# A two-block transformer kernel: joined products in a recurrence, and a reordered tail

## The reference

```python
# mixer: a matrix-memory attention group and a delta-rule recurrence, forward and backward (2 directions z)
q, k = silu(mq), silu(mk) * D_HM ** -0.5          # after a convolution
out_m = sigmoid(mo) * headnorm(mlstm(q, k, v, gates))
def step(state, inp):                              # the recurrence, per head, 512 positions
    removed = einsum('zhvk,zhk->zhv', state, kh_t)
    state = state * w_t - removed[..., None] * (kh_t * a_t) + v_t[..., None] * k_t
    return state, einsum('zhvk,zhk->zhv', state, r_t)
x = layernorm(ALPHA * x + g1 * (mixed @ w_out)) * gain + bias
h = modulate(x)                                    # another layer norm
# experts: 4 groups of 8; the best group, in it the best two experts of each token
w = softmax(two best) * p_group
# tokens sorted by expert, padded to blocks of places, each block with one expert's weights
y = (silu(xb @ gate[e]) * (xb @ up[e])) @ down[e] * w
x = layernorm(ALPHA * x + g2 * sum(y)) * gain + bias
```

## Time and profile before

| what | before |
|---|---|
| median of 3 runs | 2221.85 us (2221.75 to 2222.93) |
| the profiled execution: its own time | 2219.88 us |
| its span | 2218.1 us |
| PE, DVE, ACT, POOL busy | 94%, 38%, 22%, 11% |
| chain that ended last: PE, DVE, ACT | 41%, 5%, 2% |

### The profile page before, as it was taken

The page is one execution under the profiler, slowest core; times in us unless marked ns, Lnnn a source line. Parts: engine busy times, 40 slices in busy tenths (PEclk is TensorE's granted clock), DMA queues, the critical chain, the costliest instruction groups (busy, mean ns, idle before and its releaser), DMA issues.

```text
span 2218.1 us, 36982 instructions
## 1 busy us (share of the span) xinstructions
PE 2077.0 (94%) x15231; PEld 1402.7 (63%) x15231; DVE 834.1 (38%) x1551; ACT 480.6 (22%) x868; POOL 247.1 (11%) x229
## 2 busy tenths in 40 slices
PE   8988999999998999999899999899996899999996
PEld 5776868864776777885355555799974444444342
DVE  1388220002248622000358846534446233233324
ACT  2245100000235400000132134443332011101110
POOL 1367000000057600000000001000000000000000
PEclk9999999999999999999899999899996899999998
DMA  7422534443533254444632324300012799999993
GB/s 233 152 76 95 190 120 152 152 153 127 174 120 108 95 190 134 152 153 151 215 109 76 113 92 140 115 4 4 4 43 114 290 372 393 394 412 394 392 393 157
DMA packets 138683, 385.63 MB, mean 174 GB/s; under 512 B 16903, under 2 KB 64367, under 8 KB 127409
## 3 DMA queue, kind: packets, MB, share of 16 engines
q1 hardware_dynamic: 138545, 383.61, 46.8%
HBM read 382.54 MB, written 1.05 MB: 173 GB/s over the span
## 4 chain that ended last, share of the span: by engine, by line
PE 41%; DVE 5%; ACT 2%; issue 1%; DMA 1%; DVEq 0%; POOL 0%; ACTq 0%; POOLq 0%
PE psum L1239 9%; PE psum L2723 9%; PE psum L1973 6%; PE psum L2747 4%; PE psum L2022 3%; PE psum L2658 3%; PE psum L2001 1%; PE psum L2326 1%; PE psum L1438 1%; ACT arena L1596 1%; DVE arena L2931 1%; DVE arena L2858 1%; PE psum L2735 1%; DMA ring<-in_w_ada_dram 1%; PE psum L1254 0%
## 5 line engine op out<-in xcount | busy, mean ns | idle before, releaser
L364 PE MATMUL psum<-arena,ring 128*128 128x256 f32 x1728 | 389.1, 385 | 17.2 <-DVE arena L935 15.8
L364 PEld LDWEIGHTS psum<-arena,ring 128*128 128x128 f32 x1728 | 330.0, 192 | 73.5 <-issue 16.6
L573 PE MATMUL psum<-arena,ring 128*128 128x256 f32 (+1 forms) x1536 | 306.8, 361 | 3.2 <-ACT arena L624 3.2
L573 PEld LDWEIGHTS psum<-arena,ring 128*128 128x128 f32 x1536 | 270.5, 189 | 39.3 <-ACT arena L624 4.0
L624 ACT ACTIVATE arena<-psum 128x512 f32<-128x512 f32 (+2 forms) x116 | 63.0, 568 | 541.1 <-PE psum L573 264.0
L1973 PE MATMUL psum<-arena 64*64 64x64 f32 (+1 forms) x3808 | 149.3, 228 | 6.4 <-DVE arena L2150 3.4
L600 PE MATMUL psum<-ring,arena 128*128 128x512 f32 x352 | 151.4, 592 | 0.0
L1973 PEld LDWEIGHTS psum<-arena 64*64 64x64 f32 x3808 | 139.3, 136 | 8.8 <-issue 3.6
L1239 PE MATMUL psum<-arena,ring 128*128 128x512 f32 (+2 forms) x432 | 142.2, 489 | 0.0
L1013 DVE TENSOR_TENSOR arena<-arena,psum 128x512 f32<-128x512 f32 x22 | 15.2, 690 | 288.8 <-PE psum L573 288.8
L600 PEld LDWEIGHTS psum<-ring,arena 128*128 128x128 f32 x352 | 66.9, 190 | 83.3 <-issue 83.2
(11 more groups left out here) (407 smaller groups left out, 2625.1 us busy)
## 6 DMA issues: line engine op xcount, KB each, us to landing
ring<-in_w_in_dram SPq DMA_DIRECT2D x31, 2048.0 KB, 8.3
ring<-in_ffn_w_dram SPq DMA_DIRECT2D x46, 1024.0 KB, 5.8
arena<-in_ex_gate_dram SPq DMA_DIRECT2D x15, 2048.0 KB, 11.2
arena<-in_ex_up_dram SPq DMA_DIRECT2D x15, 2048.0 KB, 15.7
arena<-in_ex_down_dram SPq DMA_DIRECT2D x15, 2048.0 KB, 17.4
ring<-in_ex_gate_dram SPq DMA_DIRECT2D x14, 2048.0 KB, 10.4
ring<-in_ex_up_dram SPq DMA_DIRECT2D x14, 2048.0 KB, 14.8
ring<-in_ex_down_dram SPq DMA_DIRECT2D x14, 2048.0 KB, 7.7
```

The source lines that it names most:

```text
L364: ins = pe.matmul(bank[:, j, :], w[:, kc, c * P:(c + 1) * P], moving[:, kc, :], start=kc == 0, stop=kc == k - 1)
L573: ins = pe.matmul(bank[:, j, tokens], both[:, i * DC + kc, j * P:(j + 1) * P], K.xT[:, kc, tokens], start=kc == 0, stop=kc == DC - 1)
```

## The change

1. **Mid.** On ACT the two Silu come ahead of the two Sigmoid drains of `mo2`, and ahead of the wait for `kh`.
2. **wkv.** The values are transposed once for both directions (4 keys `vt`, 64 matmuls, at the start; they overwrite `rv`). The identity stands beside the right operands, so that `mr`, `m` and (for context) `nr` come with the transposes that `t1`, `t2` gave: 128 columns in place of 64 for `m` always, for `mr` and `nr` in context. `t2` is gone, and `t1` too in context. In the levels 2 to 4 (`JOINED`) one product of 128 columns gives the next power and the growth of the inverse, and DVE drains it by one addition of [0, inv]; ACT drains the transposed power (`pt`). POOL fills a zero part and a copy of `one` for each direction.
3. **Tail.** ACT writes the second diagonal early but drains the second gate rows after the first tile's `h2T`; PE makes them behind the first router. `route` is signalled when the choice is made; the weights are computed in `route_weights`, after `choose` and `owners`. PE does the counts of the first tile while the second is routed. `plan` gives the places first; `owners` (with `planned`) comes after `choose`. PE, ACT and DVE load the number of blocks only ahead of the loop, and PE does the first block's gate and up products ahead of the pair's gather.

```diff
+JOINED = range(2, LEVELS - 1)
@@ mid_scalar
-    for i in range(2):
-        drain(("mo2", i), K.mixed_gate[:, 2 * i:2 * i + 2, :], ACT.Sigmoid, ...)
...
-    act.wait_ge(K.sem["kh"], K.count("kh"))
     act.wait_ge(K.sem["conv_mk"], K.count("conv_mk"))
     act.activation(K.km, K.km, ACT.Silu).then_inc(K.sem["km"], 1)
     act.wait_ge(K.sem["conv_mq"], K.count("conv_mq"))
     act.activation(K.qm, K.qm, ACT.Silu).then_inc(K.sem["qm"], 1)
+    for i in range(2):
+        drain(("mo2", i), K.mixed_gate[:, 2 * i:2 * i + 2, :], ACT.Sigmoid, ...)
...
+    act.wait_ge(K.sem["kh"], K.count("kh"))
@@ wkv_tensor: inner
-        each(("mr", c, z), 2 if lat else 1, (t.b, kr))
-        each(("m", c, z), 1, (t.decayed(c, False)[:, :, 0, :], t.b))
-        each(("nr", c, z), 2 if lat else 1, (t.k, kr))
+        kr = t.decayed(c, True) if lat else t.decayed_and_one(c)
+        each(("mr", c, z), 2, (t.b, kr))
+        for u in range(HP):
+            for r in HEAD_ROWS:
+                ins = pe.matmul(bank[r, u], t.decayed(c, False)[r, u, 0, :], t.b_and_one(u)[r], start=True, stop=True)
+        each(("nr", c, z), 2, (t.k, kr))
@@ wkv_tensor: level
+        if n in JOINED:
+            each(("pt", n, c, z), 1, (z_now, zt_now))
...
+        if n in JOINED:
+            each(("pw", n, c, z), 2, (zt_now, t.power_and_inv(n - 1)))
+        elif n > 1:
             each(("iv", n, c, z), 1, (zt_now, t.inv))
@@ wkv_vector: grow
+        if n in JOINED:
+            ins = tt_op(t.power_and_inv(n), by_two(K.bank(key)), t.zero_and_inv, ALU.add)
@@ wkv_tensor: before the chunks
+    pe.wait_ge(K.sem["one_ready"], K.count("one_ready"))
+    for i in range(CHUNKS // 2):
+        values_turned(i)
@@ wkv_tiles_gpsimd
+        pool.memset(t.zero, 0.0).then_inc(link.sem, 1)
+        pool.wait_ge(link.sem, link.count())
+        pool.tensor_copy(t.kb_and_one[:, 2 * HP, :], K.one).then_inc(link.sem, 1)
+        pool.wait_ge(link.sem, link.count())
@@ tail_tensor
-    gate_rows(1)
     for tt in range(TT):
         token_tile_turned(tt)
         router_products(tt)
+        if tt == 0:
+            gate_rows(1)
...
+    pe.wait_ge(K.sem["route"], K.count("route", 0, 1))
+    pe.matmul(pos0, K.earlier, K.chosen[:, 0, :], start=True, stop=True)
+    pe.matmul(first, K.ones[0:1, :], K.rt_hot[0:1, 0, 1, :], start=True, stop=True).then_inc(K.full(("pos", 0)), 1)
+    pe.matmul(total, K.ones, K.chosen[:, 0, :], start=True, stop=False)
+    pe.matmul(pos1, K.ones, K.chosen[:, 0, :], start=True, stop=False)
+    pe.wait_ge(K.sem["route"], K.count("route", 0, 2))
+    pe.matmul(total, K.ones, K.chosen[:, 1, :], start=False, stop=True).then_inc(K.full(("total", 0)), 1)
+    pe.matmul(pos1, K.earlier, K.chosen[:, 1, :], start=False, stop=True).then_inc(K.full(("pos", 1)), 1)
@@ tail_scalar
+    gate_diagonals(0)
     gate_rows(0)
-    gate_rows(1)
+    gate_diagonals(1)
...
+        if tt == 0:
+            gate_rows(1)
@@ pair_tensor
-    blocks = block_count(pe, K)
...
-    pe.wait_ge(K.sem["chosen_at"], K.count("chosen_at"))
-    for q in range(2):
-        gather(q, K.bank(("first", q))).then_inc(K.full(("first", q)), 1)
...
+    pe.wait_ge(K.sem["chosen_at"], K.count("chosen_at"))
+    for q in range(2):
+        gather(q, K.bank(("first", q))).then_inc(K.full(("first", q)), 1)
...
+    blocks = block_count(pe, K)
@@ pair_vector
-    blocks = block_count(dve, K)
     choose(dve, K, link, 0, PLACES, "one_chosen")
+    owners(dve, K, more)
+    for tt in range(TT):
+        route_weights(dve, K, more, tt)
     weigh(dve, K, link, PLACES, "one_weighted")
...
+    blocks = block_count(dve, K)
```

More of the change, by code:

```diff
@@ L1171 @@
 )
-CHUNK_EVENTS = dict(wkv_tiles=1, decay=CHUNKS * ZS, hats=CHUNKS * ZS, inv_start=CHUNKS * ZS)
+CHUNK_EVENTS = dict(wkv_tiles=1, one_ready=1, decay=CHUNKS * ZS, hats=CHUNKS * ZS, inv_start=CHUNKS * ZS, strict=(CHUNKS + LAT) * ZS,
+                    pairs=LAT * ZS)
 TAIL_EVENTS = dict(
@@ L1571, in mid_scalar @@
     key_norms((2, 3))
+    act.wait_ge(K.sem["conv_mk"], K.count("conv_mk"))
+    act.activation(K.km, K.km, ACT.Silu).then_inc(K.sem["km"], 1)
+    act.wait_ge(K.sem["conv_mq"], K.count("conv_mq"))
+    act.activation(K.qm, K.qm, ACT.Silu).then_inc(K.sem["qm"], 1)
     for i in range(2):
@@ L1983, in inner, with values_turned @@
         pe.wait_ge(K.sem["hats"], turn_of(c, z))
[L1984 to L2002 removed]
+        kr = t.decayed(c, True) if lat else t.decayed_and_one(c)
+        each(("mr", c, z), 2, (t.b, kr))
+        key = ("m", c, z)
+        pe.wait_ge(K.empty(key), K.empty_count(key))
+        bank = by_two(K.bank(key))
+        for u in range(HP):
+            for r in HEAD_ROWS:
+                ins = pe.matmul(bank[r, u], t.decayed(c, False)[r, u, 0, :], t.b_and_one(u)[r], start=True, stop=True)
+        ins.then_inc(K.full(key), 1)
+        each(("nr", c, z), 2, (t.k, kr))
+    def turned(c, z):
+        t, key = K.wkv[z], ("t1", c, z)
+        pe.wait_ge(K.empty(key), K.empty_count(key))
+        bank = by_two(K.bank(key))
+        for i, src in enumerate((t.b, t.k)):
+            for u in range(HP):
+                for r in HEAD_ROWS:
+                    ins = pe.matmul(bank[r, u, i, :], src[r, u, :], one[r, :], start=True, stop=True)
+        ins.then_inc(K.full(key), 1)
+    def values_turned(i):
+        key = ("vt", i)
+        pe.wait_ge(K.empty(key), K.empty_count(key))
+        bank = by_two(K.bank(key))
+        for j in range(2):
+            at = (2 * i + j) * CH
+            for u in range(HP):
+                for r in HEAD_ROWS:
+                    ins = pe.matmul(bank[r, u, j, :], K.rv[r, u, at:at + CH], one[r, :], start=True, stop=True)
+        ins.then_inc(K.full(key), 1)
     def level(n, c, z):
@@ L2622, in plan, with owners @@
             dve.wait_ge(link.sem, link.count())
+def owners(dve, K, link):
+    tt_op, ts_op = dve.tensor_tensor, dve.tensor_scalar
+    ends = K.plan[:, 1, :]
+    n = 2 * PAIRS
+    tt_op(K.ended, K.token[:, 0:n].unsqueeze(2).broadcast_to([P, n, EXPERTS]), ends.unsqueeze(1).broadcast_to([P, n, EXPERTS]),
+          ALU.is_ge).then_inc(link.sem, 1)
+    dve.wait_ge(link.sem, link.count())
+    dve.tensor_copy(K.owner[:, n:n + 1], ends[:, EXPERTS - 1:EXPERTS])
+    dve.tensor_reduce(K.owner[:, 0:n], K.ended, AX_X, ALU.add).then_inc(link.sem, 1)
+    dve.wait_ge(link.sem, link.count())
+    ts_op(K.owner[:, 0:n], K.owner[:, 0:n], float(EXPERTS - 1), None, ALU.min).then_inc(link.sem, 1)
+    dve.wait_ge(link.sem, link.count())
+    dve.tensor_copy(K.block_expert[:, 0:n + 1], K.owner[:, 0:n + 1]).then_inc(K.sem["planned"], 1)
 def pair_sync(sp, K, A):
```

197 lines of the change are left out of this document (118 added, 79 removed).

## The result

The changed kernel takes 2190.74 us (median of 4 runs, 2188.97 to 2193.68), the kernel before 2221.8 beside it: ratio 0.9864, 95% interval 0.9847 to 0.9882. Forecast was 2194.3 with a range of 2188 to 2202. Beside the first group of experiments the same file took 2189.84 (ratio 0.9865, 0.9848 to 0.9881).

The account below looks back on a forecast made before the run. PE was taken to bound the kernel nearly everywhere, all parts lying on one chain, so savings add: six terms sum to -27.5, from 2219.88 to 2192.4 us profiled, or 2194.3 as median (1.97 above); range 2188 to 2202.

Parts of the forecast that it names:

- Mid, the step that failed: Attention group's start: Silu first ends PE's idle time and brings the first exponential sooner, ACT then pacing as before; -5.7 us.
- Recurrence start: Start of the recurrence: the value transposes' end, not POOL, sets when `inner` starts, and level 1 comes sooner; -1.1 us.
- Recurrence, chunks: Recurrence chunks: left out transposes and joined levels save 10.4 us, less 1.0 of waits for DVE; -9.4 us.
- Second gate rows: Tail: first square root 6.45 us sooner, but 4.55 lost again at the second tile; -1.9 us.
- The rival that the whole wait moves: Tail: the gate rows' wait moves whole to the second tile, total 2196.2 us; chance 0.06.
- Choice and places: Tail, second choice to first gather: fewer products, owners behind `choose`, load gone; gather sooner, -8.1 us.
- First expert: First gather to the loop: waits covered by reordering, part of the wide products at half clock; -1.3 us.
- Loop: Loop over pairs: the period stays 31.6 us, no gain.
- Wide products at twice a narrow one: Recurrence rival: a wide product costs twice a narrow one, 4.3 us more, 2198.6; chance 0.07.
- the long hand-off: Joined levels' rival: hand-off 1.5 us instead of 0.95 gives 2201.5, chance 0.09; from 1.93 on slower than before, 0.02.
- A clock that rises before the first gather and stays: First expert rival: PE's clock rises before the first gather, 5.6 us more gained, 2188.7; chance 0.08.

Follow-up runs that it names:

- second pair: Kernel before and changed kernel, each profiled a second time with no edit; the terms sum to -27.5 us.
- silu_last: Changed kernel with the two Silu behind the Sigmoid drains again: 2195.2 us, ratio 0.9893.
- rows_drained_last: Changed kernel, but ACT drains the second gate rows behind the second tile's `h2T`, bank order changed too: 2184.48 us, ratio 0.9843.
- first pair: First profiled executions of the kernel before and of the changed kernel, 2219.88 and 2188.97 us; the spans differ by 30.95.
- joins_apart: Changed kernel with recurrence levels 2 to 4 as three narrow groups each again, no joined product: 2194.5 us, ratio 0.9884.
- owners_first: Changed kernel with the owners of the blocks ahead of the places again: 2193.07 us, ratio 0.9883.
- gather_first: Changed kernel with the second gather ahead of the first expert's wide products again: 2190.33 us, ratio 0.9873.
- after_again: Second trace of the changed kernel, no edit: span 2187.1 us.
- thin filler: `rows_drained_last` plus unread products on PE in the tail's waits (4 per tile turn, 6 before second choice, 5 before first gather): 2179.32 and 2179.58 us.

## Why the prediction was right, and where its terms were off

- **Sum.** -27.5 was forecast for the profiled execution; -30.95 and -27.5 were measured in the two pairs, -31.1 and -30.3 by the medians. Every term had its sign. That the second pair meets the forecast to the tenth is luck: there mid missed by 1.8, the second gate rows by 1.1, the start by 0.4 and the choice by 0.2 one way, and the chunks (0.6), the first expert (0.9), the loop (1.4) and the stretch that nothing touched (0.5) made up for it the other way.
- **Mid, the step that failed.** "From there ACT sets the pace as before" holds for ACT (16 in 6.17) and the first exponential came 5.5 sooner for 5.7. What the step leaves out is that PE then waits for ACT (2.00 us) and makes the first values at half the clock, which before had fallen on an idle PE: 8.84 us for 7.16, 1.7 us lost, -3.9 in place of -5.7. `silu_last` shows both numbers from the other side, and in the one execution whose clock stayed (`rows_drained_last`) the term is -5.6, though the recurrence's start then took 1.5 to 2.7 us more.
- **Recurrence start.** I had the end of the transposes of the values set the start. In the first trace they ended at 1403.4 and `hats` did (PE waits 1.52 for DVE), in the second the transposes did. The clock's rise decides: -0.7 to -1.9 around the -1.1, within the bounds; in `rows_drained_last`, where it rose only at 1406.81, the same code gave +0.8, outside them.
- **Recurrence, chunks.** A wide group took 0.88, and against the second trace of before the latent chunks are 1.1 to 1.2 shorter (forecast 1.2), the context chunks 1 to 3 by 1.4, 1.6 and 2.7 (forecast 1.6). Part of the 2.7 is only the place of the count, since the next chunk's `mr` is wide in both kernels; counted from level 1 to level 1 the first four are 1.4, 1.3, 1.9 and 1.7. PE runs through the joined levels without a pause: the 1.0 us of waits for DVE that the sum set against the joins did not come. Of the 2.5 us over the forecast in the first pair 1.9 were the first execution of the kernel before; 0.6 is left; the joins, worth 2.3 by `joins_apart` where the sum had 1.6, would account for it. The left out transposes gave 7.7 where the sum had 7.9. By the Trainium skill's rule ("TensorE: Matmul & The Clock Gate", section "Back-to-back issue gap": about 60 cycles for up to 64 columns, 134 for 128) the 80 wide groups, 48 of them joins, would together have cost 13 us more, an estimate. Taking the joins apart cost 2.3 us in the recurrence, so the runs speak against the rule for this shape a second time.
- **Second gate rows.** -6.46 at the first square root, counted from its variance (forecast -6.45), or -6.2 at the first tile's transposes, counted from the recurrence's end; of this 5.0 to 5.3 were given back at the second tile (forecast 4.55, at most 6.45). The rival that the whole wait moves did not come true, but `rows_drained_last` shows that the wait was the only thing there: without it those 5.3 us come back.
- **Choice and places.** -7.9 for -8.1; nothing gained in the first tile, as laid out. `owners_first` gives the 3.4 of its own term.
- **First expert.** -1.7 and -2.2 for -1.3; the clock stayed low until 1709.1 (forecast: 4.7 us of the wide products at half rate; it was 5.0, and 3.7 in the second trace) and `gather_first` gives 1.6.
- **Loop.** "The loop's period stays 31.6" was wrong: 31.53, 0.1 less in each of 13 to 14 periods, 1.3 us. The first pair has 1.7 more from a clock dip that the kernel before showed once in two traces. The instructions of the loop are the same and its first product is not held by weights. The 0.1 us has a place: PE's wait behind ACT's copy, ahead of the products by down, is 0.29 us in every period before and 0.18 after (the first line is the kernel before):

```profile
1780.74 3.66 PE L2747 MATMUL psum<-arena 128*64 128x512 f32 x16 [0.29 <-ACT arena L2805]
```
```profile
1782.62 3.66 PE L2844 MATMUL psum<-arena 128*64 128x512 f32 x16 [0.18 <-ACT arena L2902]
```

In `joins_apart` the wait is 0.18 too, and the 0.1 us lies in the wide products at the period's end (7.20 us for 7.09). The cause of either stays open.

- **Rivals.** Wide products at twice a narrow one, and the long hand-off: excluded by 0.88 and by DVE's 0.65 of slack. A clock that rises before the first gather and stays: in neither trace of the changed kernel (in the second it was at 1.00 from 1694.71 to 1698.12, which reached 0.6 us into the gather). With filler it stayed up in two traces, and gather to loop took 25.9 and 26.7 us for the 30.4 of `after_again`: 4.5 and 3.7 less, where the rival had 5.6.

## What to carry to other kernels

A wait that is moved past one consumer falls on the next in the same queue: look for the place in the order where nobody is behind it, here behind the second tile's last ACT work (4.9 us for one moved call). Price a saving that lets PE idle elsewhere with the granted clock of the products behind it, not only with the wait. And profile the kernel before twice before a difference of 1 or 2 us is explained.

The best version measured drains the second gate rows last and has the thin filler: 2179.32 and 2179.58 in its two groups of runs, 1.7% less than before (0.9828 and 0.9829).

## What the runs showed that was not expected

- PE's idle time of 2.0 us ahead of the first values was followed by a stretch at the lower clock (1.2 GHz) in seven of the eight traces whose code is the changed kernel's up to there, and by none in one: at this place the same pause costs 1.7 us or nothing. The Trainium skill tells of a kernel in which short pauses of PE between groups of products came often enough that the clock went down and up again ("TensorE: Matmul & The Clock Gate", section "A second HAM failure mode: psum-queue depth-cycling"). Here one pause of 2.00 us stands ahead of the fall; whether repeated short ones are enough no run here shows.
- The same kernel had its first gather in 3.76 and in 6.61 us in two executions, by the clock alone.
- A filler product is only as early as the bank it writes: the same eight products cost 2.0 us at the first heads in one bank and nothing in another, and gained nothing in either.
- A clock that is kept up at one place can be down at the next: of those eight traces the one whose clock stayed up at the first heads had it down at the recurrence's start, and its level 1 lies between those of the two traces of the changed kernel.
